# Adding each expert block's result into the output rows by gather, gated add and scatter, with the experts of the four groups taken in turn

## The reference

```
xn  = rms_norm(x);  P = xn @ W_in          # six parts of 512 columns
yc  = B * causal_conv3(C * h);  ya = stick_breaking_attention(q, k, v)
x   = x + concat(rms_norm(yc), rms_norm(ya)) @ W_out
x   = x + HierMoE(rms_norm(x))
HierMoE: top-1 of 4 groups, then top-2 of the 8 experts in it (32 experts),
         gate = p_group * softmax(top two logits)
         out[token] += gate * ((silu(xb @ w1[e]) * (xb @ w3[e])) @ w2[e])
```

## Time and profile before

| | us |
|---|---|
| median of 3 runs | 1353.81 (1353.19 to 1359.11) |
| the profiled execution's own time | 1361.15 |
| its span | 1359.5 |
| PE busy | 1218.1 (90%) |
| DVE busy | 871.8 (64%) |
| ACT busy | 732.6 (54%) |
| POOL busy | 146.9 (11%) |
| HBM read, written | 252.88 MB, 25.17 MB |

### The profile page before, as it was taken

The page is one execution under the profiler, slowest core; times in us unless marked ns, Lnnn a source line. Parts: engine busy times, 40 slices in busy tenths (PEclk is TensorE's granted clock), DMA queues, the critical chain, the costliest instruction groups (busy, mean ns, idle before and its releaser), DMA issues. The chain is left out here.

```text
span 1359.5 us, 16775 instructions
## 1 busy us (share of the span) xinstructions
PE 1218.1 (90%) x5870; PEld 984.5 (72%) x5870; DVE 871.8 (64%) x910; ACT 732.6 (54%) x918; POOL 146.9 (11%) x194
## 2 busy tenths in 40 slices
PE   6999989979998998799945999999999999999930
PEld 5887767757776776588834888888888888888830
DVE  4314434445335446533264999999999999999935
ACT  5332523453354244421104788888888888888820
POOL 1000000000000003010002011111111111111000
PEclk9999969988998998899956999999999999999975
DMA  7111100100100103331064899999999999999509
GB/s 205 33 31 32 32 16 16 32 15 1 32 16 16 32 16 124 140 155 47 32 263 149 317 375 384 389 386 381 380 386 381 380 383 385 378 386 388 206 17 370
DMA packets 57339, 261.89 MB, mean 193 GB/s; under 512 B 13008, under 2 KB 33488, under 8 KB 43984
## 3 DMA queue, kind: packets, MB, share of 16 engines
q1 hardware_dynamic: 46928, 240.31, 46.4%
q0 software_dynamic: 9216, 16.80, 3.3%
q10 hardware_dynamic: 1152, 4.19, 0.8%
HBM read 252.88 MB, written 25.17 MB: 205 GB/s over the span
## 5 line engine op out<-in xcount | busy, mean ns | idle before, releaser
L1246 DVE TENSOR_TENSOR e_lo<-W,e_hi 128x1024 fp32r<-128x1024 f32 x384 | 452.6, 1220 | 25.2 <-ACT e_hi L1240 22.3
L1240 ACT ACTIVATE e_hi<-W 128x1024 fp32r<-128x1024 f32 x384 | 403.4, 1060 | 96.4 <-PE ps L1211 94.5
L731 DVE TENSOR_TENSOR_SCAN kept<-kept 128x128 f32<-128x128 f32 (+7 forms) x64 | 91.0, 1422 | 228.6 <-ACT kept L588 191.7
L1209 PE MATMUL ps<-e_hi,xT_hi 128*128 128x512 f32 x512 | 204.2, 399 | 7.1 <-DVE e_lo L1246 7.1
L1211 PE MATMUL ps<-e_lo,xT_hi 128*128 128x512 f32 x512 | 201.3, 393 | 0.0
L1210 PE MATMUL ps<-e_hi,xT_lo 128*128 128x512 f32 x512 | 200.7, 392 | 0.0
L587 ACT ACTIVATE soft<-ps,q_scale 128x128 f32<-128x128 f32 (+7 forms) x54 | 38.1, 705 | 200.4 <-PE ps L456 189.2
L407 PE MATMUL ps<-xnT_hi,w_hi 128*128 128x512 f32 x320 | 128.9, 403 | 14.4 <-DVE u L699 6.9
L407 PE MATMUL ps<-xnT_lo,w_hi 128*128 128x512 f32 x320 | 128.5, 402 | 0.0
L407 PE MATMUL ps<-xnT_hi,w_lo 128*128 128x512 f32 x320 | 128.3, 401 | 0.0
L1209 PEld LDWEIGHTS ps<-e_hi,xT_hi 128*128 128x128 f32 x512 | 97.5, 190 | 26.9 <-issue 4.0
(11 more groups left out here) (211 smaller groups left out, 1845.8 us busy)
## 6 DMA issues: line engine op xcount, KB each, us to landing
W<-in_w_dram SPq DMA_DIRECT2D x96, 2048.0 KB, 10.7
w_raw<-in_w_in_dram SPq DMA_DIRECT2D x20, 512.0 KB, 4.0
yy<-y_rows SPq DMA_DIRECT2D x8, 1024.0 KB, 13.3
xt<-in_x_dram SPq DMA_DIRECT2D x8, 512.0 KB, 3.8
w_out_raw<-in_w_out_dram SPq DMA_DIRECT2D x4, 1024.0 KB, 8.0
xn_rows<-xn SPq DMA_DIRECT2D x8, 512.0 KB, 2.6
out_dram<-x ACTq DMA_DIRECT2D x8, 512.0 KB, 8.9
x<-in_x_dram SPq DMA_DIRECT2D x1, 3072.0 KB, 13.6
```

Source lines behind the costliest of these rows:

```text
L731: dve.tensor_tensor_scan(back, back, back, 1.0, ALU.mult, ALU.min).then_inc(multiplied, 1)
L1209: pe.matmul(o, xs_hi[:, k], e_hi[:, p, cols], start=(k == 0), stop=False)
L1240: act.activation(e_hi[:, p], flat[:, p * D:(p + 1) * D], ACT.Copy).then_inc(s["hi_made"], 1)
L1246: dve.tensor_tensor(e_lo[:, p], flat[:, p * D:(p + 1) * D], e_hi[:, p], ALU.subtract).then_inc(s["lo_made"], 1)
```

## The change

Four things change together.

1. Output rows. The output projection block also stores x2 to the output (one 512 KB store a tile, put ahead of the store of xn2 on SP's queue). In the expert stage every block then gathers its 128 output rows into `acc[b]`, DVE adds gate times the down product to them, and POOL scatters the rows back to the output. `y_rows`, `act_y`, and the final block are gone. The gates come from a table in HBM, `gate_rows`, stored by SP in the router block and gathered for each block (128 single numbers).
2. Order of the experts. Since a token's two pairs lie in one group, the blocks are taken as group 0, 1, 2, 3, 0, 1, ...: block n is expert 8*(n mod 4) + n // 4. Two blocks that write the same row are thus at least four apart, and the gather of rows for block n+2 waits for the scatter of block n.
3. Engines. The copy of hidT's high part goes from DVE to ACT; the copy of y by ACT becomes the gated add on DVE (after the gate split of the block two later).
4. Overflow. The test for overflow blocks is made in 3 steps of 5 blocks instead of 15 steps of one; unused steps of a taken test point to an added empty column.

POOL's queue is in the order shown in `round_of` below. The core of the diff:

```diff
@@ output projection block, SP
                 for m in range(NT):
+                    sp.wait_ge(x2_made, 2 * m + 2)
+                    sp.dma_start(outv[m], x2[:, m]).then_inc(x2_stored, 16)
                     sp.wait_ge(xn2_made, m + 1)
                     sp.dma_start(xn2_rows_v[m], xn2[m % 2]).then_inc(xn2_stored[m % 2], 16)
+                sp.wait_ge(x2_stored, 16 * NT)
@@ router block, SP
+                with nc.allow_non_contiguous_dma(reason="one number of each pair"):
+                    sp.wait_ge(gates_made, 1)
+                    for k in range(2):
+                        sp.dma_start(gate_view[k], gate[k]).then_inc(gates_stored, 16)
+                sp.wait_ge(gates_stored, 32)
@@ router block, POOL
+                pool.memset(slot_pair[:, COLS:COLS + 1], 4 * PAIRS).then_inc(unused_cleared, 1)
+                pool.memset(slot_token[:, COLS:COLS + 1], 2 * PAIRS).then_inc(unused_cleared, 1)
@@ router block, DVE
-                link(dve.tensor_copy(over_list, ps[0:1, 3, 0:OVER + 1]))
+                link(dve.tensor_scalar(over_fill, ps[0:1, 3, 0:OVER + 1], 0.0, float(COLS), ALU.is_equal, ALU.mult))
+                link(dve.tensor_tensor(over_list, ps[0:1, 3, 0:OVER + 1], over_fill, ALU.add))
@@ helpers
         def pe_down(pe, s, n, start):
             pe.wait_ge(s["hidT_made"], n + 1)
-            pe.wait_ge(s["y_made"], n)
+            pe.wait_ge(s["added"], n)
...
-        def act_y(act, s, n, b, rounds, down_start):
-            act.wait_ge(s["freed"], used(down_start + PIECES))
-            act.wait_ge(s["scattered"][b], 16 * rounds)
-            act.activation(y[b], psf[:, 5 * BANK:7 * BANK], ACT.Copy).then_inc(s["y_made"], 1)
+        def act_hidT(act, s, n):
+            act.wait_ge(s["hid_turned"], n + 1)
+            act.activation(hidT_hi.rearrange("p k t -> p (k t)"), ps[:, 4], ACT.Copy).then_inc(s["hidT_hi_made"], 1)
+
+        def dve_add(dve, s, n, b, rounds, down_start):
+            dve.wait_ge(s["freed"], used(down_start + PIECES))
+            dve.wait_ge(s["gates_in"][b], 16 * rounds)
+            dve.wait_ge(s["rows_in"][b], 16 * rounds)
+            dve.scalar_tensor_tensor(acc[b], psf[:, 5 * BANK:7 * BANK], slot_gate[b], acc[b], ALU.mult, ALU.add).then_inc(s["added"], 1)
...
+        def pool_rows_in(pool, s, n, b, rounds, col):
             if not (isinstance(rounds, int) and rounds == 0):
                 pool.wait_ge(s["scattered"][b], 16 * rounds)
+            pool.tensor_copy(idx_pair[b], slot_pair[:, bass.ds(col, 1)]).then_inc(s["out_indexed"], 1)
+            pool.tensor_copy(idx_out[b], slot_token[:, bass.ds(col, 1)]).then_inc(s["out_indexed"], 1)
+            pool.wait_ge(s["out_indexed"], 2 * n + 2)
             start_step(pool)
+            pool.indirect_dma_start(out=slot_gate[b], out_offset=None, in_=gate_rows, ...).then_inc(s["gates_in"][b], 16)
+
+        def pool_rows_start(pool, s, b):
+            start_step(pool)
+            pool.indirect_dma_start(out=acc[b], out_offset=None, in_=out_rows, ...).then_inc(s["rows_in"][b], 16)
+
+        def pool_rows_out(pool, s, n, b):
+            pool.wait_ge(s["added"], n + 1)
+            start_step(pool)
+            pool.indirect_dma_start(out=out_rows, ..., in_=acc[b], ...).then_inc(s["scattered"][b], 16)
@@ expert stage, POOL
-                def gather_and_scatter(e, b, rounds):
-                    pool_gather(pool, s_e, e + 2, b, e + 1, rounds + 1, e + 2)
-                    pool_gather_start(pool, s_e, b, 2 * e + 2)
-                    pool_scatter(pool, s_e, e - 1, 1 - b, rounds - 1 + b, e - 1, 2 * e + 3)
...
+                for n in range(2):
+                    pool_rows_in(pool, s_e, n, n, 0, EPG * n)
+                    pool_rows_start(pool, s_e, n)
+
+                def round_of(n, r, i, rounds, gather=True):
+                    b = i % 2
+                    if gather:
+                        j, q = (i + 2, r) if i < 2 else (i - 2, r + 1)
+                        pool_gather(pool, s_e, n + 2, b, n + 1, rounds + 1, EPG * j + q)
+                        pool_gather_start(pool, s_e, b, n + 3)
+                    pool_rows_out(pool, s_e, n, b)
+                    if gather:
+                        pool_rows_in(pool, s_e, n + 2, b, rounds + 1, EPG * j + q)
+                        pool_rows_start(pool, s_e, b)
@@ expert stage, ACT and DVE
                     act_silu(act, s_e, e, gate_start(e))
                     if not (isinstance(e, int) and e == 0):
+                        act_hidT(act, s_e, e - 1)
...
                     dve_split(dve, s_e, gate_start(e), W1[b])
+                    if add_rounds is not None:
+                        dve_add(dve, s_e, e - 2, b, add_rounds, down_start(e - 2))
                     dve_split(dve, s_e, up_start(e), W3[b])
@@ overflow block
-                with eng.Fori(0, OVER) as n:
-                    with eng.If(n < n_over):
-                        body(n)
+                with eng.Fori(0, OVER // OVER_STEP) as g:
+                    with eng.If(g * OVER_STEP < n_over):
+                        for i in range(OVER_STEP):
+                            body(g * OVER_STEP + i)
```

More of the change, by code:

```diff
@@ L75, in hymba_moe_layer @@
     xn2_rows = nc.dram_tensor("xn2_rows", (S, D), F32, kind="Internal").ap()
-    y_rows = nc.dram_tensor("y_rows", (PAIRS, D), F32, kind="Internal").ap()
+    gate_rows = nc.dram_tensor("gate_rows", (PAIRS, 1), F32, kind="Internal").ap()
+    out_rows = out.rearrange("a s d -> (a s) d")
     with ExitStack() as ctx:
@@ L1171, in hymba_moe_layer @@
         hidT_lo = place("hidT_lo", [P, FT, P], F32R)
-        y = [place(f"y{i}", [P, D]) for i in range(2)]
+        acc = [place(f"acc{i}", [P, D]) for i in range(2)]
         PIECES = KT * F // D
@@ L1178, in hymba_moe_layer @@
         idx_pair = [place(f"idx_pair{i}", [P, 1], I32) for i in range(2)]
+        idx_out = [place(f"idx_out{i}", [P, 1], I32) for i in range(2)]
+        slot_gate = [place(f"slot_gate{i}", [P, 1]) for i in range(2)]
         assert KT * F == FT * D
@@ L1322, in _, with load, load_round @@
             def _(sp):
-                def load(w, wv, e, b, landed, n):
-                    sp.wait_ge(s_e["lo_made"], n + PIECES)
+                def load(w, wv, n, e, landed, start):
+                    b = n % 2
+                    sp.wait_ge(s_e["lo_made"], start + PIECES)
                     sp.dma_start(w[b], wv[bass.ds(e, 1)].rearrange("e p k f -> p (e k) f")).then_inc(expert_w[b][landed], 16)
[L1329 to L1340, removed]
+                def load_round(n, r, i):
+                    load(W1, w1_v, i, EPG * i + r, 0, gate_start(n - 2))
+                    load(W3, w3_v, i, EPG * i + r, 1, up_start(n - 2))
+                    if not (isinstance(n, int) and n == 2):
+                        j, q = (i - 1, r) if i else (NG - 1, r - 1)
+                        load(W2, w2_v, j, EPG * j + q, 2, down_start(n - 3))
+                load_round(2, 0, 2)
+                load_round(3, 0, 3)
+                with sp.Fori(1, EPG) as r:
+                    for i in range(NG):
+                        load_round(NG * r + i, r, i)
+                load(W2, w2_v, NG - 1, NE - 1, 2, down_start(NE - 3))
             @block.gpsimd
@@ L1361, in _ @@
[L1361 to L1367, removed]
+                for n in range(2):
+                    pool_gather(pool, s_e, n, n, 0, 0, EPG * n)
+                    pool_gather_start(pool, s_e, n, n + 1)
@@ new lines, in _ @@
+                for b in range(2):
+                    pool.memset(acc[b], 0.0).then_inc(cleared, 1)
+                    pool.memset(slot_gate[b], 0.0).then_inc(cleared, 1)
+                pool.wait_ge(cleared, 6)
+                for n in range(2):
+                    pool_rows_in(pool, s_e, n, n, 0, EPG * n)
[10 more added lines that the diff above has]
+                        pool_rows_start(pool, s_e, b)
@@ L1368, in _ @@
+                for i in range(NG):
+                    round_of(i, 0, i, i // 2)
+                with pool.Fori(1, EPG - 1) as r:
+                    for i in range(NG):
+                        round_of(NG * r + i, r, i, 2 * r + i // 2)
+                for i in range(NG):
+                    round_of(NE - NG + i, EPG - 1, i, NE // 2 - 2 + i // 2, gather=i < 2)
                 for b in range(2):
@@ L1393, in _, with round_of @@
             def _(act):
-                def round_of(e, b, rounds, y_rounds=None, last=False):
+                def round_of(e, b, rounds, last=False):
                     act.wait_ge(expert_w[b][0], 16 * rounds)
                     act_split(act, s_e, gate_start(e), W1[b])
-                    if y_rounds is not None:
-                        act_y(act, s_e, e - 2, b, y_rounds, down_start(e - 2))
                     act.wait_ge(expert_w[b][1], 16 * rounds)
@@ L1434, in _ @@
                 round_of(0, 0)
-                with dve.Fori(0, NE // 2 - 1) as i:
-                    round_of(2 * i + 1, 1)
-                    round_of(2 * i + 2, 0)
```

(36 more changed lines are left out.)

74 lines of the change are left out of this document (39 added, 35 removed).

## The result

The changed kernel takes 1756.5 us (median of 4 runs, 1754.22 to 1759.49) against 1356.03 (1353.19 to 1359.11): ratio 1.296 (95% interval 1.292 to 1.2995), slower by 30%. Forecast were 1756, a range of 1590 to 1870, and slower at 95%.

The account below looks back on a forecast made before the run. PE was taken to set the pace at 17.75 us a round, DMA close behind. Terms: 1361.15 + 444 - 33.8 - 10.0 + 0.6 + 0.5 + 1 = 1763.5; put on the runs' median, 1756 us, range 1590 to 1870.

Parts of the forecast that it names:

- The loop: Expert stage: x's gather queues behind the scatter's landing on POOL; round 33.0 us instead of 17.75, 29 rounds, +444 us.
- Step 1: Expert stage, from PE's turn of x to the end of DVE's gated add, at full clock: 10.15 us.
- step 6: PE's lower clock after idling for x, in the turn and products behind it: 2.1 us a round, bounds 0 to 5.9.
- Steps 2 and 3: From the scatter's operand being ready to its start, 0.87 us; then the scatter's landing beside weight loads, 7.0 us.
- Step 4: POOL's wake-up, index copies, gathers of gates and rows, and pauses up to x's gather: 5.9 us, lower end 4.2.
- Step 5: Landing of the gather of x beside weight loads: 7.0 us, between 4.1 alone and 13.0 loaded.
- rival C: Landings as in the full pipeline, scatter 9.2 and x 13.0 us: round 41.2, time 1992 us; chance 5%.
- The sum of the stage: Expert stage: a round of 33.0 us in place of 17.75, over 29 rounds +444 us.
- the tail: End of the expert stage: add for y +0.3 us, second to last scatter closer to the last +0.3 us.
- Overflow: Overflow test at the end: some 0.83 us a step, so 3 steps instead of 15 save 10.0 us.
- Router: Router block: two more memsets and one more tiny DVE step, +0.5 us; gate stores taken as 0.
- Rival D: Expert stage: x lands before PE wants it, DMA's 18.1 us sets the round, 1322 us; chance 3%.

Follow-up runs that it names:

- e2: Changed kernel with POOL's gather of x issued four blocks ahead, behind the scatter and ahead of the wait for its landing: 1364.3 us, ratio 1.0055.
- e3: Kernel before with only POOL's queue in the changed order (gather x of n+2, scatter n, wait for its landing): 1758.6 us, ratio 1.295.
- e4: Changed kernel with 48 unused products more a round on PE, ahead of its wait for x: 1726.7 us, ratio 1.272.
- e7: Changed kernel with a quarter of each load of weights from block 2 on: 1635.0 us, ratio 1.205.
- e11: Changed kernel with loads of weights from block 2 on cut to 16 rows of 2 KB: 1594.8 us, ratio 1.176.
- e1: Changed kernel with POOL's gather of x three blocks ahead, right behind the scatter and ahead of the wait for its landing: 1593.8 us, ratio 1.174.
- e6: e2 with three buffers instead of two for output rows, gates and indices, so POOL waits for a scatter a round old: 1354.0 us, ratio 0.998.
- e10: e6 with 128 numbers a row instead of 1024 in the gather of rows, taken from the table of xn2: 1324.6 us, ratio 0.976.

## Why the prediction was right

- **The loop**, with its two landings, its place and its 29 rounds: shown, by the 29 waits of PE for x, by e2 (loop opened, 392 us gone) and by e3 (loop put into the old kernel, 401 us added).
- **Step 1 with step 6** (turn to end of add): forecast 10.15 + 2.1 = 12.25, measured 11.8 in the round shown and 12.1 on average over the 29 (11.4 to 12.9). e4 shows that the clock part is real: it recovered 1.6 a round of the 2.0. The 4.4 us of slow products in the earlier trace rows stood behind a second pause of 3.60; in the loop it is the slow turn and the few products behind it that together cost 2.0.
- **Steps 2 and 3**: 0.87 and 7.0, measured 0.91 and 7.1. That 7.0 was a choice between 3.2 and 9.2; e7 and e11 show both its floor and that the loads make the rest.
- **Step 4**: 5.9, measured 5.5. The pause ahead of an indirect DMA is 0.85 to 0.9 behind an index copy or a wait for another engine; behind another DMA it is 0.3. I had seen only the first two kinds. The lower end, 4.2, takes away two pauses, but only the row gather stands right behind another DMA, so the sum without its pause is 5.1 and the lower end of the round 23.4, not 22.5; step 6's upper end, 5.9, adds up to 5.8. Neither changes the forecast.
- **Step 5**: 7.0, measured 7.1. Right, partly by luck: e1 and e3, where x is issued at about the moment of a load and not 3 us after it, had 11.2 and 10.6, toward rival C's 13.0.
- **The sum of the stage**: 33.0 a round against 32.6 on average (some 33 and some 32). The stage with its tail was forecast at 444.6 and measured 439.1, and that is two errors: the 29 rounds came 12 us short (432), and the tail, for which I had taken 0.6, came to 6, since I had not seen that the last down product would wait 7.5 us for the add.
- **Overflow**: the term that was mis-sized. I divided nearly all of 13.1 us by 15 steps (0.83) and left 0.7 outside; it is 0.49 a step and 5.8 outside. -10.0 was forecast; to the end of the span 7.4 are left of 13.1, so -5.7. This and the stage's 5 us cancel, and the first half varied by 8 us, so the agreement to 1 us is chance.
- **Router**: +0.5 forecast, +0.6 measured. Final block -33.8: gone as forecast. The stores of x2 can't be seen within the 8 us by which the first half varied.
- **Rival D's price** (DMA at 18.1 sets the round, 1322) is where the prediction is weakest. With the queue mended the kernel stood at 1354 (e6), not 1322: late transfers do not stretch rounds evenly by 0.3 us but make single rounds slip by up to 4 us, since a wait of 2 us was followed by the lower clock in five of ten cases. It is e10, at 1324.6, that stands where rival D put the open loop.
- The clock was 0.79 in the round shown, and at 1.2 GHz for the turn and the first two to nine products after each of the 29 waits for x. The rule of the Trainium skill that I weighed ("TensorE: Matmul & The Clock Gate", "Loop structure matters more than you think") held in this trace. The fit of the Trainium skill for the two landings on the page "DMA: Bandwidth & Descriptors", section "Anatomy of one DMA — SWDGE (gpsimd) path", an estimate of 2.6 us for 0.26 MB, was below even e11, where scatter and x took 3.3 and 4.5 with hardly a load beside them.

## What to carry to other kernels

Before moving a wait on an in-order queue, write out what stands behind it and ask when that is wanted; a landing put ahead of a prefetch turns the prefetch into latency once a round, whatever the engines' busy shares say. Here a gather had to be issued both ahead of the wait for this round's scatter and a round before its result was wanted: e1 did only the first and stayed at 1594, e2 did both and came to 1364. What is written back needs buffers enough that the wait is for an old scatter (here three). And count bytes by stage, not in total: 8.4 MB went from an end where nothing else ran into a stage with 98% busy DMA engines. Of the 39.5 us that the end gave, e6 lost 31 to late rounds, most of them by e10 for these bytes, and 6 to the last down product's wait.

## What the runs showed of the hardware that I had not expected

- At the same mean share of the DMA engines (55% in the changed kernel, 52 to 56% in e3) the gather of x, 0.26 MB, landed in 7.1 us when issued 3 us after a 2 MB load and in 10.6 when issued with one; with loads of 32 to 64 KB it took 4.5. The kernels differ in more than this phase, so that the phase is the cause is not shown.
- The length of a pause of PE did not tell whether the lower clock would follow. In e4 it followed six pauses of 2.00 to 3.12 us, one of them the 2.33 above, and not those of 2.54, 2.89 and 3.05; in the kernel before it did not follow one of 2.73 us (at 1301.8).
- An indirect DMA right behind another on POOL starts 0.3 us after that one's instruction ends; behind an index copy, 0.85.
